# The last channel chunk of a depthwise convolution moves from VectorE to GpSimd

## The reference

```
def conformer_conv(a, g, w_dw, b_dw, ln_g, ln_b):
    u = a * sigmoid(g)                      # 512 tokens x 512 channels
    u = depthwise_causal_conv(u, w_dw) + b_dw     # 31 taps per channel
    mu, var = mean(u, channels), mean((u - mu)**2, channels)
    un = (u - mu) * rsqrt(var + LN_EPS) * ln_g + ln_b
    return silu(un)
...
mixed = concatenate([attn_out, conv_out]);  h = h + mixed @ w_out
```

## Time and profile before

| | |
|---|---|
| median of 3 runs | 1922.59 us (1922.33 to 1922.96) |
| the profiled execution, its own time | 1921.71 us |
| its span | 1919.9 us |
| granted clock of PE, mean over the span | 0.98 of full speed |
| PE, PEld busy | 1833.1 us (95%), 1465.9 us (76%) |
| DVE busy | 1105.2 us (58%) |
| ACT busy | 754.6 us (39%) |
| POOL busy | 114.7 us (6%) |

### The profile page before, as it was taken

How to read it: one execution, slowest core, us unless ns; L and a number is a source line. 1 busy time by engine, 2 the same in 40 slices (tenths; PEclk the granted TensorE clock), 3 DMA queues, 4 the chain that set the end, 5 groups by cost and what they waited for, 6 DMA issues and landing times.

```text
span 1919.9 us, 23479 instructions
## 1 busy us (share of the span) xinstructions
PE 1833.1 (95%) x8886; PEld 1465.9 (76%) x8886; DVE 1105.2 (58%) x1664; ACT 754.6 (39%) x1089; POOL 114.7 (6%) x114
## 2 busy tenths in 40 slices
PE   5987999999999989989999999999978999999998
PEld 4874788888887777768888888877755788888886
DVE  5889444444333665554676763347998266766422
ACT  4225443333223224453544542222257354445321
POOL 0000010000021100531000000100000100000000
PEclk9997999999999999989999999999989999999999
DMA  4430032323232411112222232332110122232321
GB/s 157 151 108 3 25 107 87 109 87 102 95 110 91 151 66 45 48 42 69 107 94 103 87 109 90 108 121 88 66 45 1 45 94 104 87 109 87 108 89 66
DMA packets 25719, 166.24 MB, mean 87 GB/s; under 512 B 3082, under 2 KB 3210, under 8 KB 6704
## 3 DMA queue, kind: packets, MB, share of 16 engines
q1 hardware_dynamic: 23328, 158.83, 24.1%
q0 software_dynamic: 1744, 5.37, 0.9%
q10 hardware_dynamic: 576, 1.05, 0.1%
HBM read 163.10 MB, written 2.13 MB: 86 GB/s over the span
## 4 chain that ended last, share of the span: by engine, by line
PE 88%; DVE 6%; issue 2%; ACT 2%; DMA 0%; DVEq 0%; SPq 0%; ACTq 0%
PE ps L394 25%; PE ps L396 25%; PE ps L395 25%; PE ps L554 1%; DVE cacc L1309 1%; PE ps L535 1%; PE ps L577 1%; PE ps L409 1%; PE ps L408 1%; PE ps L407 1%; DVE ring L1363 1%; ACT ring L936 1%; ACT w_hi L789 1%; PE ps L613 1%; DVE tmp L1372 1%
## 5 line engine op out<-in xcount | busy, mean ns | idle before, releaser
L394 PE MATMUL ps<-a_hi,w_hi 128*128 128x512 f32 x1616 | 636.6, 394 | 8.2 <-DVE a_lo L1138 3.8
L396 PE MATMUL ps<-a_hi,w_lo 128*128 128x512 f32 x1616 | 629.7, 390 | 0.0
L395 PE MATMUL ps<-a_lo,w_hi 128*128 128x512 f32 x1616 | 629.4, 389 | 0.0
L394 PEld LDWEIGHTS ps<-a_hi,w_hi 128*128 128x128 f32 x1616 | 303.7, 188 | 84.0 <-issue 17.4
L395 PEld LDWEIGHTS ps<-a_lo,w_hi 128*128 128x128 f32 x1616 | 303.7, 188 | 65.1 <-issue 2.6
L396 PEld LDWEIGHTS ps<-a_hi,w_lo 128*128 128x128 f32 x1616 | 303.6, 188 | 63.7
L1132 DVE TENSOR_TENSOR w_lo<-raw,w_hi 128x2048 fp32r<-128x2048 f32 x82 | 192.4, 2346 | 247.6 <-ACT w_hi L789 247.6
L789 ACT CAST w_hi<-raw 128x2048 fp32r<-128x2048 f32 x82 | 156.0, 1902 | 350.5 <-PE ps L396 298.2
L394 PE MATMUL ps<-h_hi,w_hi 128*128 128x512 f32 x528 | 206.2, 391 | 0.0
L396 PE MATMUL ps<-h_hi,w_lo 128*128 128x512 f32 x528 | 205.4, 389 | 0.0
L395 PE MATMUL ps<-h_lo,w_hi 128*128 128x512 f32 x528 | 205.4, 389 | 0.0
(11 more groups left out here) (214 smaller groups left out, 2009.8 us busy)
## 6 DMA issues: line engine op xcount, KB each, us to landing
raw<-weights_dram SPq DMA_DIRECT2D x148, 1024.0 KB, 4.8
bias_t<-bias_rows_scratch POOLq DMA_DIRECT2D x8, 256.0 KB, 7.1
ncb<-decay_rows_scratch POOLq DMA_DIRECT2D x8, 256.0 KB, 5.0
out_dram<-xT SPq DMA_DIRECT2D x8, 256.0 KB, 2.0
xT<-x_in_dram ACTq DMA_DIRECT2D x4, 256.0 KB, 6.1
xT<-x_in_dram SPq DMA_DIRECT2D x4, 256.0 KB, 8.7
vec<-vectors_dram SPq DMA_DIRECT2D x1, 282.5 KB, 3.6
ring<-ramp_dram POOLq DMA_DIRECT2D x1, 260.0 KB, 5.4
```

Of the source, the lines that this page charges most:

```text
L394: pe.matmul(dst, wh, hi[:, k0 + k, :], start=start and k == 0, stop=False)
L395: pe.matmul(dst, wh, lo[:, k0 + k, :], start=False, stop=False)
L396: last = pe.matmul(dst, wl, hi[:, k0 + k, :], start=False, stop=stop and k == nk - 1)
```

## The change

GpSimd forms the last channel chunk (chunk 3) by itself, in its own queue right behind the bias transfers: once for tap 0 a product with the bias added, then for each of the 30 other taps a product into a spare tile (`tmp[:, 1]` and `tmp[:, 2]` in turn) and a sum of that tile into `cacc[:, 3, :]`. That is 61 instructions. A new semaphore, `taps3`, counts them: a sum waits for its product, and a product waits for the sum that read its tile two taps ago. VectorE's table holds the other three chunks, 93 taps, so 31 instructions go. PE waits for `taps3` ahead of the fourth matmul of the sum over the channels.

```
@@ gpsimd, behind the bias transfers @@
+            wait("glu", 4)
+            nc.gpsimd.tensor_scalar(cacc[:, 3, :], cu[:, 3, 0:S], col("conv_w", 3 * TAPS), col("conv_b", 3),
+                                    ALU.mult, ALU.add).then_inc(sem["taps3"], 1)
+            for j in range(1, TAPS):
+                if j > 2:
+                    wait("taps3", 2 * (j - 2) + 1)
+                nc.gpsimd.tensor_scalar(tmp[:, 1 + j % 2, :], cu[:, 3, j:j + S], col("conv_w", 3 * TAPS + j), None, ALU.mult
+                                        ).then_inc(sem["taps3"], 1)
+                wait("taps3", 2 * j)
+                nc.gpsimd.tensor_tensor(cacc[:, 3, :], cacc[:, 3, :], tmp[:, 1 + j % 2, :], ALU.add
+                                        ).then_inc(sem["taps3"], 1)
@@ tensor, the sum over the channels @@
-            wait("taps", 4 * TAPS)
+            wait("taps", 3 * TAPS)
             for c in range(4):
+                if c == 3:
+                    wait("taps3", 2 * TAPS - 1)
@@ vector, the table and the function that issues the taps @@
-            for lo, hi, n in ((0, 1, 9), (0, 2, 9), (0, 3, 9), (0, 4, 4 * TAPS - 27)):
+            for lo, hi, n in ((0, 1, 9), (0, 2, 9), (0, 3, 3 * TAPS - 18)):
...
-                    if k == 4 * TAPS:
+                    if k == 3 * TAPS:
```

More of the change, by code:

```diff
@@ L176 @@
     "lin", "fconv", "fstep", "silu", "h", "hhi", "hlo",
-    "pad", "glu_g", "glu", "taps", "ln_sum", "ln_act", "ln_dve", "brow_mm", "brow_ev", "masks",
+    "pad", "glu_g", "glu", "taps", "taps3", "ln_sum", "ln_act", "ln_dve", "brow_mm", "brow_ev", "masks",
     "rope_dve", "rope_act",
```

## The result

| | before | after |
|---|---|---|
| median of 4 runs each | 1922.66 us (1922.33 to 1922.96) | 1936.66 us (1936.07 to 1937.66) |
| ratio, 95% interval | | 1.0077 (1.0065 to 1.0089) |
| span of the profiled execution | 1919.9 us | 1934.8 us |
| VectorE busy | 1105.2 us | 1124.2 us |
| GpSimd busy | 114.7 us | 228.8 us |

What follows compares the result with a forecast made beforehand. VectorE was taken to bound nearly all of the chain up to 193 us. The profiled 1921.71 us + 26.4 (late attention) - 9.8 (groups 2 and 3) gave 1938.3, forecast as 1939, range 1916 to 1947.

Steps and rivals of the forecast that it cites:

- The turn: Projection: one GpSimd product and sum go by per three VectorE taps, 3.54 us, so 1.18 us a tap.
- `w_lo`: Projection: VectorE's seven subtractions for it are held up like taps, each growing by 0.52 to 2.73 us.
- the first step: From 70.45 us to the attention: VectorE, held up by GpSimd, arrives at 170.9, not 144.5, 26.4 us later.
- PE's waits: Projection: `w_lo` comes late and PE waits 3 us per slab from about the fourth on; VectorE stays the bound.
- The first group: Attention's first four units: five left GpSimd pairs and six taps make 14.0 us against 13.8, counted as 0.
- Groups 2 and 3: Attention: without taps each falls from 15.0 to 10.1 us, as in the kernel's last attention, gaining 9.8 us.
- The last stretch: From 192.89 us on: it has one tap now and PE ends it, so the gain is 0.
- (a): Rival, no loss: VectorE isn't held up where its queue is full, attention starts at 144.5; 1908 us, chance 0.13.
- (b): Rival, milder turn: a sum keeps VectorE off for half its length, a tap 1.0 us; 1924 us, chance 0.22.
- (c): Rival: VectorE keeps its place, GpSimd starves, and PE waits for the fourth chunk, + 22; 1945 us, chance 0.12.
- The estimate by the Trainium skill's rate for one input: With 0.5 us a product, all 30 pairs fall ahead of the attention and the sum comes 8 us higher.

Runs made afterwards that it cites:

- the faster product: The changed kernel with each GpSimd product given a second operation (+ 0.0): 1940.45 us, ratio 1.0098 against the kernel before.
- the 14 taps in the attention: GpSimd forms only the last 14 taps of chunk 3, from the attention on, VectorE 110: 1930.26 us, ratio 1.0041 against the kernel before.
- the kernel with nine taps: GpSimd forms only chunk 3's last 9 taps, behind VectorE's last tap, with two-operation products: 1919.44 us, ratio 0.9986 against the kernel before.

## Why the prediction was right, and where its terms were off

The mechanism held: not the new wait, the table or GpSimd's own length, but GpSimd's sums in VectorE's way. With only the sums gone the loss is gone, and with only GpSimd's work added it is there. That the time came so near the forecast is in part luck: two terms were wrong by 5 to 6 us each, in opposite directions. By the steps:

- **The turn.** Predicted 3.54 us for three taps, 1.18 each; measured 3.47 and 1.157.
- **`w_lo`.** Predicted to grow to 2.73 us, measured 2.28. This is the mis-sized term of the first step: 7 x 0.45 = 3.2 us, and the tap's 69 x 0.023 = 1.6 more. 26.4 - 3.2 - 1.6 = 21.6; measured from 144.51 to 166.82, less the 0.96 us by which everything in this execution starts later (the last `cu` product ends at 71.41, not 70.45), 21.35. Beside sums alone it does grow. In the full turn it never meets a sum that is under way: at 101.11 it starts 0.48 us behind a product, at 86.82 the sum starts 0.49 us behind it, and in both it is GpSimd that waits. These two cases alternate in the seven subtractions.
- **PE's waits.** Predicted 3 us a slab from about the fourth on. The weight loads waited for `w_lo` 1.2, 2.9 and 2.7 us in slabs 7, 8 and 9, the fourth to sixth. Right in the place, at or under the size, and none of it counts: the chain that ended last goes through VectorE's taps there.
- **The first group: the step that failed.** It was put at 0 (14.0 against 13.8). From the first row of the attention to the second group's 512-key row it took 24.3 us, 144.51 to 162.87 = 18.4 before: + 5.9. I had let the group be as long as VectorE's work in it. But VectorE also waits there, 3.4 us in all, 3.29 of them for PE at the group's end, and it did so (3.1 us) in the run without products and sums, whose group is 13.6 us. And I had given the scalings 1 us of waits for GpSimd. Beside its last pairs eight scalings took 5.4 us, against 2.8 without GpSimd's work, and six taps 6.6, against 4.1: 5.1 us more, of the 5.3 between the two groups (18.9 and 13.6). The long pause of PE ahead of the group (20.3 us) isn't needed for it: with GpSimd's work all in the attention PE's longest was 5.3 us, and the group took 18.1. PE's granted clock stands at 0.5 from 147 to 171 and from 174 to 191 us, so the PE work that ends the group, 185.56 to 191.03, takes 5.5 us, where the same matmuls take 3.0 in the next group. How much shorter the group would be at full clock was not tested.
- **Groups 2 and 3.** 10.1 us each, as the last attention had said: - 9.8, exact.
- **The last stretch and the rest.** Put at 0. The last stretch took 11.6 us, 1.5 less. Later another 2.1 us went, in work that the change leaves alone: 1.1 near 700 us and 2.7 in the second layer's attention, where before shows two stretches at half clock (834 to 841 and 848 to 855) and after one, less 1.6 lost near 1430 us, where after runs at half clock for 17 us and before for 13.6. Why these stretches fall otherwise wasn't tested. Against before, other executions differ there by up to 3 us as well (the one with sums alone by 2.9), so differences of that size between two traces say nothing of the change.

The sum: + 1.0 + 21.4 + 5.9 - 9.8 - 1.5 - 2.1 = + 14.9, which is 1934.8 - 1919.9. Against + 16.6 predicted, a first term that was 5.0 too large and one of + 5.9 that was put at 0 nearly cancel.

Of the rivals, (a) fails on the taps of 1.157 us, (b) on the turn, which gives the sum all of its length, and (c) on the wait for chunk 3, which is not there: GpSimd's last sum starts at 186.42, and PE asks at 219.2. The Trainium skill's rule on the shared interface ("Advanced Engine Details and Errata", GpSimd Details) agrees with the runs, and they give it a size here: 30 us for 61 instructions.

The estimate by the Trainium skill's rate for one input ("GPSIMD Engine Reference", Engine selection), 8 us above the row's sum, found a test only in part, in the faster product (1.55 us beside VectorE, against that estimate's 0.5). It came out 3.8 us slower, with all pairs ahead of the attention, as that estimate had it, but with 7.2 us given back in the attention up to the second group, which it had not.

## What to carry to other kernels

Before work is given to an engine that looks idle, count how long its instructions hold what it shares with the busy one. Here a tap on GpSimd holds VectorE off for 1.5 us (3.47 - 2.0, products and sums together) to save it 0.66, so by these numbers no share of GpSimd's pays beside a full VectorE queue, and the 14 taps in the attention lost too. The only placement that gained here, by under 0.2%, has the sums where VectorE has no taps left. Products alone cost nothing in slabs with 2 us of room. A stretch relieved of its bound gets as fast as the next one allows, and a like stretch elsewhere in the trace gave that time exactly, where no clock was low.

## What the runs showed of the hardware that was not expected

- GpSimd's product with two operations (multiply, add 0.0) on 128x512 took 0.69 us where nothing was beside it (at 199.41 us in the kernel with nine taps), and 1.55 on the mean beside the full queue; the product with one operation takes 1.57 us and 2.23. Tap 0, which has two, took 0.98 us beside VectorE's taps and 0.76 in the attention.
- The alternation is regular: 1.78, 1.17 and 0.74 us for three taps, again and again over 70 us. `w_lo` kept its 2.28 us in it, and the GpSimd instruction started beside it took 2.9 to 4.1 us. Beside sums alone `w_lo` took up to 3.38.
- A scaling on VectorE is lengthened as well: eight of them took 5.4 to 6.1 us beside GpSimd's pairs and 2.7 to 2.8 without.
